# Product-key picks made head by head between the query weights, with each head's rows gathered when its picks are known

## The reference

```
def peer(h, w_pq, sub_keys, u_tab, v_tab):          # h: tokens x 2048
    qr = (h @ w_pq).reshape(t, 8 heads, 2, 128)
    sc = einsum('thpd,hpnd->thpn', qr, sub_keys)     # 8 heads x 2 halves x 128 keys
    s_top, i_top = top_k(sc, 16)
    cand = s_top[..., 0, :, None] + s_top[..., 1, None, :]
    c_top, c_pos = top_k(cand.reshape(t, 8, 256), 16)
    expert = i_top[0][c_pos // 16] * 128 + i_top[1][c_pos % 16]
    g = softmax(c_top)
    a = gelu(einsum('thkd,td->thk', u_tab[expert], h))
    return einsum('thk,thkd->td', g * a, v_tab[expert])
```

## Time and profile before

| what | value |
|---|---|
| median of three runs | 1708.07 us |
| profiled execution | 1710.41 us, span 1708.4 us |
| TensorE busy | 1667.7 us, 98% |
| VectorE busy | 1022.4 us, 60% |
| ScalarE, GpSimd busy | 404.7 us, 247.3 us |
| data moved | 569.77 MB, mean 334 GB/s |
| granted TensorE clock | 0.995 |
| gathered rows, median to landing | 21.9 us (first table), 26.4 us (second) |

### The profile page before, as it was taken

The page is one execution under the profiler, slowest core; times in us unless marked ns, Lnnn a source line. Parts: engine busy times, 40 slices in busy tenths (PEclk is TensorE's granted clock), DMA queues, the critical chain, the costliest instruction groups (busy, mean ns, idle before and its releaser), DMA issues.

```text
span 1708.4 us, 28369 instructions
## 1 busy us (share of the span) xinstructions
PE 1667.7 (98%) x11296; PEld 1585.1 (93%) x11296; DVE 1022.4 (60%) x1688; ACT 404.7 (24%) x1019; POOL 247.3 (14%) x250
## 2 busy tenths in 40 slices
PE   7999999999999999999999999999989999999999
PEld 5768888887999999999999999999989999999998
DVE  5426695765547999767777777736435334443444
ACT  6547567646542000022112111200000000000000
POOL 1020000000001031222212112203113111111110
PEclk9999999999999999999999999999999999999999
DMA  9664446466556699899999999999999999999997
GB/s 337 231 146 133 138 127 195 146 224 222 168 177 234 238 367 410 348 421 421 422 422 422 422 422 422 422 402 381 422 412 421 422 422 422 422 421 422 422 421 295
DMA packets 106373, 569.77 MB, mean 334 GB/s; under 512 B 11088, under 2 KB 13264, under 8 KB 47376
## 3 DMA queue, kind: packets, MB, share of 16 engines
q1 hardware_dynamic: 56480, 216.51, 34.5%
q0 software_dynamic: 31696, 220.50, 32.0%
q10 hardware_dynamic: 18144, 132.13, 18.9%
HBM read 563.04 MB, written 4.46 MB: 332 GB/s over the span
## 4 chain that ended last, share of the span: by engine, by line
PE 62%; DMA 22%; DVE 12%; issue 3%; ACT 1%; POOL 0%; SPq 0%; DVEq 0%; ACTq 0%
PE ps L1472 32%; DMA late<-in_u_rows,sel 18%; PE ps L1219 5%; PE ps L1221 5%; PE ps L1220 5%; PE ps L1417 4%; PE ps L1238 2%; PE ps L1375 2%; PE ps L1374 2%; PE ps L1373 2%; DVE late L1081 2%; DMA raw<-in_w_in 1%; DMA raw<-in_v_tab 1%; DVE w_lo L778 1%; DVE acts L1057 1%
## 5 line engine op out<-in xcount | busy, mean ns | idle before, releaser
L1085 DVE SCALAR_TENSOR_TENSOR acts<-late,sel,acts 128x2048 f32<-128x2048 f32 x77 | 181.1, 2351 | 246.9 <-DMA late<-in_v_tab,sel 246.0
L1472 PE MATMUL ps<-acts,raw 128*128 (+1 forms) x2048 | 285.3, 300 | 6.6 <-DMA raw<-in_v_tab 6.6
L1417 PE MATMUL ps<-acts,late 128*128 128x160 f32 x2048 | 288.4, 300 | 0.0
L1472 PEld LDWEIGHTS ps<-acts,raw 128*128 128x128 f32 x2048 | 281.7, 191 | 6.8 <-issue 6.8
L1417 PE MATMUL ps<-acts,raw 128*128 128x160 f32 x2048 | 286.6, 299 | 0.0
L1472 PE MATMUL ps<-acts,late 128*128 (+1 forms) x2048 | 284.2, 299 | 0.0
L778 DVE TENSOR_TENSOR w_lo<-raw,w_hi 128x512 fp32r<-128x512 f32 (+1 forms) x288 | 188.9, 682 | 159.0 <-ACT w_hi L518 158.1
L1417 PEld LDWEIGHTS ps<-acts,late 128*128 128x128 f32 x2048 | 282.2, 191 | 0.0
L1417 PEld LDWEIGHTS ps<-acts,raw 128*128 128x128 f32 x2048 | 280.5, 190 | 0.0
L1472 PEld LDWEIGHTS ps<-acts,late 128*128 128x128 f32 x2048 | 280.1, 190 | 0.1
L1081 DVE SCALAR_TENSOR_TENSOR late<-late,acts 128x2048 f32<-128x2048 f32 x76 | 173.8, 2290 | 79.3 <-DMA late<-in_u_rows,sel 79.0
(11 more groups left out here) (208 smaller groups left out, 1494.3 us busy)
## 6 DMA issues: line engine op xcount, KB each, us to landing
raw<-in_w_in SPq DMA_DIRECT2D x72, 512.0 KB, 3.7
raw<-in_u_tab SPq DMA_DIRECT2D x33, 1024.0 KB, 9.3
late<-in_u_tab SPq DMA_DIRECT2D x33, 1024.0 KB, 9.3
raw<-in_v_tab SPq DMA_DIRECT2D x32, 1024.0 KB, 10.0
raw<-in_v_tab ACTq DMA_DIRECT2D x32, 1024.0 KB, 10.0
late<-in_v_tab SPq DMA_DIRECT2D x32, 1024.0 KB, 10.0
late<-in_v_tab ACTq DMA_DIRECT2D x32, 1024.0 KB, 10.0
raw<-in_u_tab ACTq DMA_DIRECT2D x31, 1024.0 KB, 9.5
```

Of the source, the lines that this page charges most:

```text
L1085: V.scalar_tensor_tensor(acc, row[n % NROW], w_sp[:, n - N_OWN:n - N_OWN + 1], acc, ALU.mult, ALU.add).then_inc(row_used, 1)
L1417: ins = mm(ps[:, q, 0:N_DN], ring[q][:, k * P:k * P + P], hF[:, k, :], start=k == 0, stop=k == KD - 1)
L1472: ins = mm(ps[:, pair_bank(k // 2), at:at + N_DN], ring[q][:, k * P:k * P + P], acts[:, ds(i * (4 * N_DN) + q * N_DN, N_DN)], start=first ...
```

## The change

Heads get an order, `HEAD_ORDER` = 6, 7, 0, 1, ... 5, and the host orders the query weights and the keys so. Scores are made per head, inside the projection: after chunks 2, 4, ... 14 TensorE makes those of the head before, and after the last chunk those of the last head. ScalarE's and VectorE's lists for the projection are written out, no longer loops. VectorE makes the splits of units 4 to 7, and then three heads' picks (6, 7 and 0 of the first block) with one half split after each of the 14 steps and two more at the end, which makes the 48 remaining ones. It computes `idx` after each head. The query rows for the sparse tokens (`hs`) follow then. Every further head, the five of the first block and the eight of the second, is followed by two rows, and the last by six more.

GpSimd issues gather 0 after `hs` is made and gather 1 on after the last query weights are used. Before rows 0, 16, 32, 48, 64 and 80 it copies the lent numbers of 16 rows and waits for that copy. The score and pick buffers move, so that the first fill covers 8704 columns and the fourth is gone; gathers up to number 28 no longer wait for `slot_ready` of all heads. The GELU of the sparse products moves to unit 120 of the first table, their scaling to unit 122, and five rows of the second table are used before unit 127.

```
--- before.py
+++ after.py
+        HEAD_ORDER = [(h + 6) % NH for h in range(NH)]
+        N_AHEAD = 3
...
             def gather(n):
+                if n == 0:
+                    pool.wait_ge(hs_ready, 2)
+                if n == 1:
+                    pool.wait_ge(piece_used, 2 * B_U)
...
+            def lend_picks(h):
+                pool.wait_ge(idx_ready, N_AHEAD + h)
+                at = N_OWN + TOPK * (h % 2)
+                pool.dma_start(idx[helpers, TOPK * h:TOPK * h + TOPK], idx[lenders[h // 2], at:at + TOPK]).then_inc(idx_in, 16)
+                pool.wait_ge(idx_in, 16 * (h + 1))
+
+            def gathers(first, end):
+                for n in range(first, end):
+                    if n < N_OWN and n % TOPK == 0:
+                        lend_picks(n // TOPK)
+                    gather(n)
+
             pool.dma_start(acc, io["x2_scratch"][0:P, :]).then_inc(acc_in, 16)
+            gathers(0, 1)
             pool.wait_ge(hs_ready, 2)
             for i in range(2):
                 pool.dma_start(hs[i][helpers, :], hs[i][lenders[i], :]).then_inc(hs_in, 16)
-            pool.wait_ge(score_done, 8)
-            pool.memset(region(A_ONES, A_TK - A_ONES), 1.0).then_inc(ones_set, 1)
+            gathers(1, NROW)
+            pool.wait_ge(score_done, 2 * NH)
+            pool.memset(region(A_ONES, A_SCORE - A_ONES), 1.0).then_inc(ones_set, 1)
+            gathers(NROW, NROW + 8)
             pool.wait_ge(slot_ready, NH)
             pool.memset(region(A_SCORE, 2048), 1.0).then_inc(ones_set, 1)
-            pool.wait_ge(idx_ready, 1)
...
-            for n in range(NROW + 8):
-                gather(n)
+            gathers(NROW + 8, NROW + 24)
             pool.wait_ge(slot_ready, 2 * NH)
             pool.memset(region(A_SCORE + 2048, 2048), 1.0).then_inc(ones_set, 1)
-            for n in range(NROW + 8, NROW + 16):
-                gather(n)
+            gathers(NROW + 24, NROW + 31)
             pool.wait_ge(gsp_ready, 1)
...
+            for u in range(2, U_PQ):
+                split_hi(B_PQ + u, u)
+                if u % 2 and u >= 3:
+                    queries_out((u - 3) // 2)
+                if u >= 7 and u % 4 == 3:
+                    scores_out((u - 7) // 4)
+            queries_out(15)
+            scores_out(NH - 1)
...
+                if c == NKEY - 8:
+                    act.wait_ge(row_used, N_OWN)
+                    nc.scalar.activation(a_sel, a_sel, ACT.Gelu).then_inc(a_done, 1)
...
+            for hp in range(N_AHEAD):
+                top_k(0, hp, weights_low)
+                row_numbers(hp)
+                weights_low()
+                weights_low()
...
+            for hp in range(N_AHEAD, NH):
+                top_k(0, hp)
+                row_numbers(hp)
+                next_row(2)
+            for hp in range(NH):
+                top_k(1, hp)
+                next_row(2)
             next_row(6)
...
+                if c == NKEY - 6:
+                    dve.wait_ge(a_done, 1)
+                    dve.wait_ge(gsp_in, 48)
+                    V.tensor_tensor(w_sp[:, 0:N_OWN], a_sel, w_sp[:, 0:N_OWN], ALU.mult).then_inc(w_ready, 1)
...
+                if c > NKEY - 6:
+                    next_row()
...
+            for c in range(16):
+                if c >= 2:
+                    pe.wait_ge(qr_done, c - 1)
+                for j in range(4):
+                    if c < 2:
+                        rest_of_norm(4 * c + j)
+                    wide_piece(c // 2, B_PQ, 4 * (c % 2) + j, c % 2)
+                if c == 2:
+                    pe.wait_ge(subk_in, 16)
+                if c >= 2 and c % 2 == 0:
+                    head_scores(c // 2 - 1)
+            head_scores(NH - 1)
```

More of the change, by code:

```diff
@@ L483, in _ @@
                 pool.dma_start(w_sp[helpers, N_TURN * i:N_TURN * i + N_TURN], w_sp[rows, N_OWN:N_PICK]).then_inc(gsp_in, 16)
[L484 to L487, removed]
             pool.wait_ge(row_used, N_TURN)
             pool.dma_start(hs[0][helpers, :], hs[0][lenders[2], :]).then_inc(hs_in, 16)
-            for n in range(N_TURN + NROW - 1, N_OWN + N_TURN + NROW - 1):
-                gather(n)
+            gathers(N_TURN + NROW - 1, N_OWN + N_TURN + NROW - 1)
             for i in range(2):
@@ L494, in _ @@
                 pool.dma_start(lent[lenders[i], :], acc_copy[helpers, :]).then_inc(lent_in, 16)
-                for n in range(N_OWN + (i + 1) * N_TURN + NROW - 1, min(N_OWN + (i + 2) * N_TURN + NROW - 1, 2 * N_OWN)):
-                    gather(n)
+                gathers(N_OWN + (i + 1) * N_TURN + NROW - 1, min(N_OWN + (i + 2) * N_TURN + NROW - 1, 2 * N_OWN))
             pool.wait_ge(row_used, 2 * N_OWN)
@@ L687, in _, with queries_out, scores_out @@
                 norm_hi(1, G_FFN, k)
[L690 to L713, removed]
+            def queries_out(c):
+                act.wait_ge(piece_used, 2 * B_PQ + 4 * c + 4)
+                nc.scalar.activation(qr[:, c, :], ps[:, c % 2, 0:SEQ], ACT.Copy).then_inc(qr_done, 1)
+            def scores_out(hp):
+                for b in range(TT):
+                    g = TT * hp + b
+                    act.wait_ge(score_mm, g + 1)
+                    nc.scalar.activation(score[b][:, 2 * hp:2 * hp + 2, :], ps[:, 2 + g % 4, 0:2 * P].rearrange("p (c n) -> p c n", c=2),
+                                         ACT.Copy).then_inc(score_done, 1)
+            for u in range(2, U_PQ):
[6 more added lines that the diff above has]
+            scores_out(NH - 1)
             act.wait_ge(x2_stored, 16)
@@ L775, in split_lo, with split_lo_half @@
                 for half in range(2):
[L776 to L779, removed]
+                    split_lo_half(u, j, half, w)
+            def split_lo_half(u, j, half, w=PIECE):
+                dve.wait_ge(hi_done, u * 2 + (half + 1))
+                slot_no = (2 * j + half) % NPART
+                V.tensor_tensor(wlo[slot_no][:, 0:w], raw[j % NRAW][:, half * w:half * w + w], whi[slot_no][:, 0:w].bitcast(F32),
+                                ALU.subtract).then_inc(lo_done, 1)
             def norm_sum(nth):
@@ L1023, in _ @@
                                     ALU.add).then_inc(hF_done, 1)
[L1024 to L1034, removed]
+            for u in range(4, 8):
+                split_lo(B_PQ + u, u)
             steps = [0]
@@ L1376, in wide_piece @@
                 ins.then_inc(piece_used, 1)
-            def wide_pair(i, base, out_done, before=lambda piece: None):
-                for c in range(2):
-                    if not (isinstance(i, int) and i == 0):
-                        pe.wait_ge(out_done, i * 2 + (c - 1))
-                    for j in range(4):
-                        before(4 * c + j)
-                        wide_piece(i, base, 4 * c + j, c)
             def rest_of_norm(piece):
@@ L1391, in rest_of_norm, with head_scores @@
                     pe.wait_ge(hTlo_done, KD + 4 * piece + 4)
[L1392 to L1405 removed]
+            def head_scores(hp):
+                pe.wait_ge(qr_done, 2 * hp + 2)
+                for b in range(TT):
+                    g = TT * hp + b
+                    if g >= 4:
+                        pe.wait_ge(score_done, g - 3)
+                    for i in range(2):
+                        c = 2 * hp + i
+                        ins = mm(ps[:, 2 + g % 4, i * P:i * P + P], qr[:, c, b * P:b * P + P], subk[:, c, :], start=True, stop=True)
+                    ins.then_inc(score_mm, 1)
+            for c in range(16):
[10 more added lines that the diff above has]
+            head_scores(NH - 1)
             pe.wait_ge(hF_done, 4)
@@ L1529 @@
     columns = lambda g: g.reshape(-1, 128).T
+    by_head = [(c + 12) % 16 for c in range(16)]
     sent = {
```

104 lines of the change are left out of this document (54 added, 50 removed).

## The result

The changed kernel takes 1710.36 us (median of 20 runs), the kernel before 1706.89 us on the same terms: a ratio of 1.0019, 95% interval 1.0013 to 1.0026. It is slower by about 3.3 us by the ratio (3.5 by the medians); 1704 was forecast. The kernel before had read 1708.07 us from three runs, and its profiled execution, 1710.41 us, was a long one: 3.5 us more than the later median. The profiled execution of the changed kernel was 1709.63 us.

What follows compares the result with a forecast made beforehand. TensorE, busy 98%, was taken as the bound, with a DMA-bound stretch in the first table. +0.7 - 6.0 - (12.0 - 10.4) + 3 = -3.9 against the profiled 1710.41 gives 1706.5, or 1704 at the median; range 1695 to 1714.

Steps and rivals of the forecast that it cites:

- What bounds the kernel: First table: TensorE, busy 98%; the DMA sets the pace from unit 65 to 119; at most 18.0 us can return.
- Scores between the weights: End of the query projection: the last head must wait for its own queries; cost 0.7 us, between 0 and 1.5.
- Picks between the splits: Query projection: VectorE needs 20.8 us where TensorE spends 24.8, so its idle time hides the picks; cost 0.
- First gathers and the fill: After the query rows: first gather at 524.5, 84 us earlier; fill 7.4 us, holding the fourth head about 6.5.
- Gates' start: Units 49 to 53: rows 32 to 35 land in time, the 6.0 us loss goes; bounds 0 to 6.
- lent indices: Copies before rows 48, 64 and 80 drain the gathers: 1 us each, 3 in all; bounds 0 and 6 each.
- The row-bound stretch and the drains: From about unit 58 to 111 the DMA leads: 10.4 us lost instead of 12.0, plus 3 us for drained queues.
- Second table: Five rows move before unit 127, last row ends near 1645; wait behind x2 rows stays: 0, between -8 and +3.
- Gates still start late: Rows 33 to 35 land 5 us later than reckoned and the same losses remain: 1709; chance 0.08.
- The second rival: At rows 48, 64 and 80 the next row comes 6 us late; at 5 us a drain, 1716; chance 0.15.

Runs made afterwards that it cites:

- the rows spread: The changed kernel with its four drains, but after unit 52 no row is used at every ninth unit: 1697.16 us, 0.9945 of the kernel before.
- second profile of the changed kernel: The changed kernel itself, unaltered, run and profiled again beside the other experiments: 1709.21 us, 1.0015 of the kernel before.
- late reload: The changed kernel, but GpSimd reloads the x2 rows after the last gathered row, SyncE no longer does: 1701.32 us, 0.9965 of the kernel before.

## Why the prediction was wrong

- *What bounds the kernel.* Right: TensorE paced by its unit loads, 18 us lost in the first table, a DMA-bound stretch. All four causes (drains, volume in the stretch, reload, rows at the gates' start) could be removed one by one, and 25 us came back.
- *Scores between the weights.* Right: +0.7 forecast, 102.74 - 102.05 = 0.69 measured, 0.5 of it the wait for the last queries.
- *Picks between the splits.* Right: the projection took no longer than its 0.69 us more; the query rows end at 519.9 us, in a profile that had started 3.5 us earlier (forecast 524.5).
- *First gathers and the fill.* Right: the fill took 7.37 us (7.4 forecast) and the fourth head's picks 15.2 instead of 9.0 us (row numbers at 535.30, first step at 520.13; its last small step alone took 6.19 us beside the fill instead of 0.23), 6.2 where 6.5 was forecast.
- *Gates' start.* **This is the step that failed.** It forecast 6.0 us back, most of the whole gain; the profiles give 0.9, -0.1 and -0.5. With 0 in place of the 6.0 the forecast's own sum is 0.7 - 1.6 + 3 = +2.1, against the 3.3 to 3.5 measured. Rows 32 to 35 were to land at 732, 737, 742 and 748 with use at 738 and on. Row 32 was used in time, but rows 33 and 34 were used as they landed, at 742.18 and 747.92, in a profile that runs 3.5 us early: 745.7 and 751.4 on the forecast's clock, some 9 us after the forecast landings. What held them is the copy before row 32: GpSimd waited 16.28 us for it, so these four gathers were issued from 728.11 on (731.6 on the forecast's clock), about when the first of them was to land. The prediction's working on the lent indices names six copies and gives a price to three, those of rows 48, 64 and 80; row 32's, right at the gates' start, it put at nothing without a reason. Without that drain the start lost only 1.1 and 1.6 us, so 4.4 to 4.9 of the 6.0 did come back. But they were then not a gain: with none of these drains the stretch lost 14.1 us instead of the 10.4 forecast, and the ratio was 0.9992 where the forecast's sum without drains, -6.9, is 0.996. The terms were added as if independent, and while the stretch is bound, what the start gives back the stretch mostly takes. The premise was wrong too: the hold on the gathers was not the cause before. And of the 6.0 us before, 4.0 were the wait and 0.1 its gate group; 1.7 were the unit behind, which took 6.19 us instead of 4.51.
- *The row-bound stretch and the drains.* Forecast 10.4 + 3 = 13.4 lost; 15.2, 12.3 and 16.8 measured. The mechanism held, but the lead of 2 us at row 37 was not there: without drains 14.1 were lost, and VectorE waited for every row from 33 to 49. The price of 1 us a drain was near: 2.9 us for three in this kernel by the ratios, 5.6 in the kernel before, and the bound of 6 each was not reached.
- *Second table.* Right in price: the wait stayed, 5.86 us, and TensorE's end did not follow the rows. The last row ended at 1653 us, 1657 on the forecast's clock, 12 us after the 1645 forecast; nothing waited for it.
- *The rivals.* "Gates still start late" is what happened; its 1709 is 1 us over the median of three, and the measured kernel is 3.3 to 3.5 over. It got 0.08, because four landing times worked out to the microsecond were trusted though they shared one source. The second rival had the place right, and the row too: row 48 came 6.25 us late, and TensorE lost 7.4 us there. But it took that for the price, and the drains of rows 48, 64 and 80 together cost 2.9 us here and 5.6 in the kernel before, 1 to 1.9 each and not 5. It rested on an estimate from the rule of turns in the Trainium skill, DMA: Bandwidth & Descriptors, section Queues, rings and completion order: by equal turns a lone gather would keep only its third. The traces agree with how late the row is, 6.25 us where that estimate gives 6; they do not with 6 as the price of a drain over the whole kernel.

What stays open: why the stretch's loss differs by up to 4 us between executions of the same schedule, and where the last 1 to 2 us of the measured 3.3 to 3.5 stand.

## What to carry to other kernels

Moving gathers earlier did not help here, where one row per unit was still asked of a memory system that could give 0.93 (4.79 / 2.485 - 1, an estimate from the rates above): the request rate of the bound stretch had to fall below capacity, so the rows saved had to be spread over its whole length. Two losses in front of the same full memory system must not be added: what one gives back the other can take. A small copy that a queue's owner waits for drains the whole queue in front of it. In a bound stretch that cost 1 to 2 us each; where a deadline follows and nothing is bound behind it (row 32 with the rows spread) it cost 4 to 5. Issued together and long before their use, the copies held up nothing. A side load goes where the memory system is no longer full, here behind the last gather.

## What the runs showed of the hardware

A small copy behind up to five gathers kept GpSimd waiting for 14 to 24 us in the kernels whose stretch is bound, and for 11 to 17 us with the rows spread; with nothing in front it was 2.70 us.

TensorE's clock made some waits dearer than they were long. In the changed kernel the gate group after the wait of 4.19 us took 2.08 us instead of 1.05, and the unit behind it 6.59 instead of 4.51; the window from 831 to 841 us has the granted clock at 0.66 of full, between its level of 1.2 GHz and that of 2.4:

```profile
833.53 6.59 PE L1461 MATMUL ps<-acts,late 128*128 128x160 f32 x32
```

```profile
831.00:841.00 10.00, 9.34 (x48) 9.34 (x49) 7.66 (x10) 1.54 (x7) 2.08 (x2) 0.66 1.01 424
```

That adds 1.03 + 2.08 = 3.1 us to the 4.19: the 7.4 us lost between units 64 and 67 (840.16 - 817.92 = 22.24 us, where 3 x 4.345 + 2 x 0.89 = 14.8 would do). The second profile of the changed kernel has such groups at the gates' start and, after a wait of 5.07 us, at 913.21:

```profile
750.01 2.07 PE L1477 MATMUL ps<-early 128*128 128x128 f32 x8 [4.23 <-ACT early L737]
...
913.21 2.08 PE L1477 MATMUL ps<-early 128*128 128x128 f32 x8 [5.07 <-ACT early L737]
```

The slow part does not always begin in the gate group. Behind the 4.02 us wait of the kernel before and the 2.99 us one above, the group took 1.16 us but the unit after it 6.19 instead of 4.51. The length of the wait alone does not decide it: one of 2.40 us had a slow group behind it (2.07 us, late reload, at 832.88), one of 2.38 us (changed kernel, at 993.24) a group of 1.16 and a unit of 4.51. So part of the spread between executions may be the clock: that was not tested.
